# A RetNet and FoX decoder step on one core: value rows folded per head, state pairs spread over the value, head and gate steps

## What is computed

```python
def retention_mixer(h, pos, S0, w_in, w_out):
    q, k, v, g = split(h @ w_in)               # 1024, 1024, 2048, 2048 columns
    q, k = rotary(q, pos), rotary(k, pos) * RET_DK ** -0.5
    ...
    inner = einsum('bhij,bjhv->bihv', einsum('bihd,bjhd->bhij', q, k) * decay, v)
    cross = einsum('bihd,bhdv->bihv', q * q_dec, S)
    S_new = exp(L * log_gamma) * S + einsum('bjhd,bjhv->bhdv', k * k_dec, v)
    o = inner + cross
    ...
    o = o * rsqrt(mean(o * o) + EPS)           # over the 512 values of a head
    return (o * silu(g)) @ w_out, S_new
```

## Time and profile before

| what | us |
|---|---|
| median of 3 runs | 1557.9 |
| lowest and highest run | 1551.91, 1560.46 |
| the profiled execution, its time | 1551.63 |
| the profiled execution, its span | 1549.6 |
| start and modulation, until the q/k slots | 0 to 48.7 |
| q/k slots | 48.7 to 105.7 |
| value slots | 105.7 to 170.5 |
| value fold and past sums | 170.5 to 183.0 |
| heads | 183.0 to 273.6 |
| gate stage | 273.6 to 361.8 |
| modulation slots of `m0c` | 361.8 to 376.6 |
| output projection | from 376.6 |

### The profile page before, as it was taken

How to read it: one execution, slowest core, us unless ns; L and a number is a source line. 1 busy time by engine, 2 the same in 40 slices (tenths; PEclk the granted TensorE clock), 3 DMA queues, 4 the chain that set the end, 5 groups by cost and what they waited for, 6 DMA issues and landing times.

```text
span 1549.6 us, 19019 instructions
## 1 busy us (share of the span) xinstructions
PE 1373.4 (89%) x6290; PEld 748.9 (48%) x6290; DVE 634.6 (41%) x1678; ACT 244.4 (16%) x516; POOL 121.9 (8%) x234
## 2 busy tenths in 40 slices
PE   5999865988988999999899879989889889999995
PEld 3787532656864443434576723323324644334343
DVE  1220333331034344444400187687781253535354
ACT  2000233321022000000210121121220130000001
POOL 3330131320000000000000001111110000000000
PEclk8999986998998999999899956696799979999998
DMA  9764264997474999999953346666663629999992
GB/s 378 298 217 154 83 243 178 351 393 313 155 317 186 391 406 405 408 405 414 401 213 123 116 163 218 225 249 226 242 229 128 271 109 364 398 408 405 399 413 108
DMA packets 77032, 430.16 MB, mean 278 GB/s; under 512 B 9832, under 2 KB 11128, under 8 KB 38432
## 3 DMA queue, kind: packets, MB, share of 16 engines
q1 hardware_dynamic: 52704, 347.72, 57.1%
q0 software_dynamic: 23200, 76.10, 13.7%
q10 hardware_dynamic: 1056, 5.36, 0.9%
HBM read 406.94 MB, written 22.20 MB: 277 GB/s over the span
## 4 chain that ended last, share of the span: by engine, by line
PE 62%; DVE 9%; DMA 5%; issue 3%; ACT 2%; DVEq 1%; POOL 0%; SPq 0%; POOLq 0%
PE bank L778 60%; DMA ring<-wstream 3%; DVE arena L2107 2%; DVE arena L1943 1%; DVE h L2103 1%; DMA arena<-state 1%; PE bank L834 1%; DVE x L1959 1%; DVEq L1938 1%; DMA xn<-v_rows 1%; ACT arena L1492 1%; DVE arena L1972 1%; ACT xn L1381 0%; PE bank L792 0%; PE bank L1297 0%
## 5 line engine op out<-in xcount | busy, mean ns | idle before, releaser
L778 PE MATMUL bank<-arena 128*128 128x264 f32 (+7 forms) x1216 | 405.3, 518 | 61.4 <-ACT arena L1363 30.1
L778 PE MATMUL bank<-ring,arena 128*64 128x512 f32 (+3 forms) x1856 | 390.8, 560 | 7.6 <-issue 5.8
L778 PEld LDWEIGHTS bank<-arena 128*128 128x128 f32 (+4 forms) x1216 | 168.7, 166 | 274.9 <-issue 171.5
L778 PEld LDWEIGHTS bank<-ring,arena 128*64 128x64 f32 (+3 forms) x1856 | 141.9, 137 | 237.5 <-issue 213.8
L1363 ACT ACTIVATE arena<-bank 128x512 f32<-128x512 f32 (+6 forms) x186 | 85.8, 471 | 531.1 <-PE bank L778 432.1
L778 PE MATMUL bank<-h,ring 128*128 128x264 f32 x640 | 149.0, 394 | 0.5 <-DMA ring<-wstream 0.5
L778 PEld LDWEIGHTS bank<-h,ring 128*128 128x128 f32 x640 | 122.6, 193 | 30.1 <-issue 9.3
L1959 DVE SCALAR_TENSOR_TENSOR x<-bank,mod,x 128x256 f32<-128x256 f32 x256 | 119.3, 475 | 0.0
L778 PE MATMUL bank<-arena,ring 128*128 128x264 f32 x512 | 117.3, 393 | 0.8 <-DVE arena L2186 0.8
L778 PE MATMUL bank<-arena,cst 16*128 16x128 f32 (+8 forms) x210 | 82.2, 503 | 32.3 <-DVE arena L2168 19.9
L778 PEld LDWEIGHTS bank<-arena,ring 128*128 128x128 f32 x512 | 98.9, 194 | 18.7 <-DVE arena L2186 0.9
(11 more groups left out here) (229 smaller groups left out, 865.2 us busy)
## 6 DMA issues: line engine op xcount, KB each, us to landing
ring<-wstream SPq DMA_DIRECT2D x296, 1024.0 KB, 8.5
arena<-vcache POOLq DMA_DIRECT2D x64, 512.0 KB, 5.2
arena<-kcache SPq DMA_DIRECT2D x64, 512.0 KB, 4.7
arena<-state POOLq DMA_DIRECT2D x32, 512.0 KB, 9.4
ss_out<-arena POOLq DMA_DIRECT2D x32, 512.0 KB, 8.6
xn<-v_rows POOLq DMA_DIRECT2D x32, 256.0 KB, 8.8
sp_out<-arena ACTq DMA_DIRECT2D x4, 512.0 KB, 2.7
cst<-consts SPq DMA_DIRECT2D x1, 2005.5 KB, 22.2
```

Of the source, the lines that this page charges most:

```text
L778: ins = nc.tensor.matmul(out, w, rhs, start=start, stop=stop, skip_group_check=True)
```

## The change

- The value rows of the samples are folded per head (`("vfold", hd)`), behind the prompt values of slots 2, 4 and 6 of the stage and after the last, and are stored per head; `vpart` shrinks to one head, and `vb` has three buffers instead of four, so POOL issues the broadcast of u + 3 behind the store of u.
- The past sums move from behind the value stage to behind its first slot.
- Pairs 0 to 3 are read behind value slots 4 to 7 (`AT_V`, counted from 0), pairs 4 to 11 in the heads (`AT_HEAD`), pairs 12 to 15 in the first four gate steps (`AT_G`). ACT's scaling moves along: pairs 0 to 5 in the value stage, one pair ahead of `head_root` and one behind it in each head, pairs 14 and 15 in the gate stage.
- DVE updates the second pair of a head behind `head_scale`, no longer ahead of it.
- `outputs_turn` of head 0 stands ahead of head 1's scores, that of head 1 in head 2, the others in gate steps 0 and 4; the samples' norm is taken in gate step 5.
- At the start the small tensors are issued ahead of x, and the rest of the constants behind slot 11. POOL's first state loads wait for the first row of `m0b`.

```diff
+AT_V = {4: 0, 5: 1, 6: 2, 7: 3}
+AT_HEAD = {0: (4, 5), 1: (6, 7), 2: (8, 9), 3: (10, 11)}
+AT_G = {0: 12, 1: 13, 2: 14, 3: 15}
...
-        t.add(("vs", i), (X0, X1)[i % 2])
-    t.add("vfold", X0)
-    t.add(("past", 0), X0)
-    t.add(("past", 1), X1)
-    t.add("past_total", X0)
+        if i and i % 2 == 0:
+            t.add(("vfold", i // 2 - 1), X0)
+        t.add(("vs", i), X2)
+        if i == 0:
+            t.add(("past", 0), X0)
+            t.add(("past", 1), X2)
+            t.add("past_total", X0)
+        if AT_V.get(i) == 0:
+            t.add(("os", 0), X1)
+    t.add(("vfold", 3), X0)
...
-        root_o = rot.rearrange("p a b -> p (a b)")[:, 2 * T:2 * T + 2 * TP].rearrange("p (r n) -> p r n", r=2)
+        osb = rot.rearrange("p a b -> p (a b)")[:, RV:2 * RV]
+        root_o = ret.take(1, TP)
         vr = rot.rearrange("p a b -> p (a b)")[:, 0:RV]
-        vb = xn[:, :, :].rearrange("p a b -> p (a b)")[:, 0:4 * RV].rearrange("p (r n) -> p r n", r=4)
+        vb = xn[:, :, :].rearrange("p a b -> p (a b)")[:, RV:4 * RV].rearrange("p (r n) -> p r n", r=3)
...
+            sp.dma_start(cst[:, 0:N_EARLY], consts[:, 0:N_EARLY]).then_inc(consts_in, 16)
+            sp.dma_start(vec[:], vecs).then_inc(consts_in, 16)
             sp.dma_start(x[:], x_in).then_inc(x_loaded, 16)
-            sp.dma_start(cst[:, 0:N_EARLY], consts[:, 0:N_EARLY]).then_inc(consts_in, 16)
             for r in range(R):
                 sp.dma_start(ring[:, r, :], wstream[r]).then_inc(slot_in[r], 16)
-                if r == 0:
-                    sp.dma_start(vec[:], vecs).then_inc(consts_in, 16)
-            sp.dma_start(cst[:, N_EARLY:], consts[:, N_EARLY:]).then_inc(rest_in, 16)
-            sp.dma_start(wsm[:], wsmall).then_inc(rest_in, 16)
+            def rest_of_constants():
+                sp.dma_start(cst[:, N_EARLY:], consts[:, N_EARLY:]).then_inc(rest_in, 16)
+                sp.dma_start(wsm[:], wsmall).then_inc(rest_in, 16)
...
-            stream(R, S_MOE0 + 3 * NE)
+            for n in range(R, S_RET):
+                sp.wait_ge(slot_used, n - R + 1)
+                sp.dma_start(ring[:, n % R, :], wstream[n]).then_inc(slot_in[n % R], 16)
+            rest_of_constants()
+            stream(S_RET, S_MOE0 + 3 * NE)
...
+            moved(pool, ("row", "m0b", 0))
             for u in range(SB):
                 pool.dma_start(st[:, u, :, :], state[state_of(u)]).then_inc(state_in[u], 16)
 
+            def store_values(hd):
+                moved(pool, ("vfold", hd))
+                pool.dma_start(v_rows[hd], vr[MW * hd:MW * hd + NS, :]).then_inc(v_stored, 16)
+
             def values_everywhere(u):
-                pool.dma_start(vb[:, u % 4, :], v_rows[u // NS, u % NS:u % NS + 1, :].to_broadcast([P, RV])) \
-                    .then_inc(vb_in[u % 4], 16)
-
-            moved(pool, "vfold")
-            for hd in range(RH):
-                pool.dma_start(v_rows[hd], vr[MW * hd:MW * hd + NS, :]).then_inc(v_stored, 16)
-            pool.wait_ge(v_stored, 16 * RH)
-            for u in range(4):
+                if u % NS == 0:
+                    pool.wait_ge(v_stored, 16 * (u // NS + 1))
+                pool.dma_start(vb[:, u % 3, :], v_rows[u // NS, u % NS:u % NS + 1, :].to_broadcast([P, RV])) \
+                    .then_inc(vb_in[u % 3], 16)
+
+            store_values(0)
+            for u in range(3):
                 values_everywhere(u)
             for u in range(NS * RH):
 
@@ -691,12 +708,14 @@
                 else:
                     pool.wait_ge(state_read, 3 * (u // NS) + u // 2 % 4 + 1)
                 pool.dma_start(ss_out[state_of(u)], st[:, u % SB, :, :]).then_inc(state_out[u % SB], 16)
-                if u + 4 < NS * RH:
-                    values_everywhere(u + 4)
+                if u + 3 < NS * RH:
+                    values_everywhere(u + 3)
                 nxt = u + 5
                 if SB <= nxt < NS * RH:
                     pool.wait_ge(state_out[nxt % SB], 16 * (nxt // SB))
                     pool.dma_start(st[:, nxt % SB, :, :], state[state_of(nxt)]).then_inc(state_in[nxt % SB], 16)
+                if u % NS == 3 and u // NS + 1 < RH:
+                    store_values(u // NS + 1)
 
...
+                    mm(ps[:], ones, prev[:, i * 512:(i + 1) * 512], False, True, full)
+                ps, full = begin("past_total")
+                mm(ps[:, 0:NS * FH], ones, past_sum.rearrange("p b h -> p (b h)"), True, True, full)
+
             pe.wait_ge(hs_ready, 1)
             for i in range(8):
                 take_slot(S_RET + 8 + i)
                 values("v", None, S_RET + 8 + i, h, i)
+                if i and i % 2 == 0:
+                    fold_values(i // 2 - 1)
                 samples_in(("vs", i), S_RET + 8 + i)
-                mm(ps[MW * hd:MW * hd + MW, :], c_("fold"), vpart[:, hd * RV:(hd + 1) * RV], True, True,
-                   full if hd == RH - 1 else None)
-            pe.wait_ge(rest_in, 32)
...
+                if i == 0:
+                    past_sums()
+                if i in AT_V:
+                    read_states(AT_V[i])
+            fold_values(3)
...
             head_scores(0)
+            outputs_turn(0)
             for hd in range(RH):
                 if hd + 1 < RH:
                     head_scores(hd + 1)
                 head_output(hd)
                 if hd == 2:
-                    outputs_turn(0)
-                read_states(2 * hd)
+                    outputs_turn(1)
+                read_states(AT_HEAD[hd][0])
                 head_norm(hd)
-                read_states(2 * hd + 1)
+                if len(AT_HEAD[hd]) > 1:
+                    read_states(AT_HEAD[hd][1])
...
-                if i in (0, 4, 7):
-                    outputs_turn({0: 1, 4: 2, 7: 3}[i])
-                if i == 6:
-                    read_states(14)
+                if i in (0, 4):
+                    outputs_turn({0: 2, 4: 3}[i])
+                if i == 5:
+                    samples_norm()
                 columns(("g", i, 1), n, 1, h)
-                if i < 7:
-                    read_states(8 + i if i < 6 else 15)
-
-            mods("m0c", 0, 2)
...
+            def scale_pair(p):
+                scale_state(2 * p)
+                scale_state(2 * p + 1)
+
+            for i in range(8):
+                for c in range(2):
+                    ps = result(act, ("v", i, c))
+                    copy(vtok[:, c, i * 256:(i + 1) * 256], ps[:, 0:256]).then_inc(free(("v", i, c)), 1)
+                if i >= 2:
+                    scale_pair(i - 2)
+            sample_rows(0)
...
                 for s in range(2):
                     ps = result(act, ("rs", hd, s))
                     copy(sp_sb[:, s, :], ps[:]).then_inc(free(("rs", hd, s)), 1)
+                scale_pair(6 + 2 * hd)
                 moved(act, ("rs", hd, 1))
                 act.dma_start(sp_out[hd], sp_sb).then_inc(sp_stored, 16)
-                if hd >= 2:
-                    act.wait_ge(o_scaled, hd - 1)
+                if hd:
+                    act.wait_ge(o_scaled, hd)
                 head_root(hd)
-                for u in range(4 * hd + 4, min(4 * hd + 8, 18)):
-                    scale_state(u)
                 if hd == 1:
-                    act.wait_ge(v_stored, 16 * RH)
-                    sample_rows(0)
-            sample_rows(1)
+                    sample_rows(1)
+                scale_pair(7 + 2 * hd)
+            sample_rows(2)
...
+                if i < 2:
+                    scale_pair(14 + i)
                 if i == 3:
-                    sample_rows(2)
-                if i == 6:
                     sample_rows(3)
+                if i == 5:
+                    root_s = norm_s[:, 0, :, :]
+                    moved(act, "sam_norm")
+                    nc.scalar.activation(root_s, root_s, ACT.Sqrt, bias=eps, scale=1.0 / RV).then_inc(sam_rooted, 1)
+            mods("m0c")
...
+            def move_states(p):
+                for u in (2 * p, 2 * p + 1):
+                    hd, b = u // NS, u % NS
+                    dve.wait_ge(vb_in[u % 3], 16 * (u // 3 + 1))
+                    dve.wait_ge(state_scaled, u + 1)
+                    for s in range(2):
+                        ins = stt(st[:, u % SB, s, :], vb[:, u % 3, :], qk[:, 8 + 2 * hd + s, TP + b:TP + b + 1],
+                                  st[:, u % SB, s, :], ALU.mult, ALU.add)
+                    ins.then_inc(state_moved, 1)
...
+            for i in range(8):
+                if i and i % 2 == 0:
+                    rows_out(i // 2 - 1)
+                ps = result(dve, ("vs", i))
+                nc.vector.tensor_copy(vpart[:, i % 2 * 256:i % 2 * 256 + 256], ps[:, 0:256]).then_inc(free(("vs", i)), 1)
+                if i + 1 in AT_V:
+                    move_states(AT_V[i + 1])
+            rows_out(3)
...
             head_in(0)
+            samples_out(0)
             for hd in range(RH):
                 if hd + 1 < RH:
                     head_in(hd + 1)
```

(17 more changed lines are left out.)

186 lines of the change are left out of this document (80 added, 106 removed).

## The result

The changed kernel takes 1625.84 us (median of 4 runs, 1618.79 to 1630.18) against 1557.08 us before (4 runs): the ratio is 1.0438, with an interval of 1.0409 to 1.0467. It is slower, as forecast, but by 69 us and not by 50; 1625.84 lies 1.8 us above the upper end of the range. The profiled execution took 1618.79 us, its span is 1616.8.

The account below looks back on a forecast made before the run. TensorE, busy 89% of the span, was taken as the bound, so its idle time shows. Terms 1.5 + 0 + 11 + 59.6 - 12 - 8.6 - 1 = +50.5 us on 1551.6 gave 1602, as median 1608; range 1576 to 1624.

Parts of the forecast that it names:

- start, to the value stage: Reordered first transfers: q/k slots start at 48.7 again, but PE idles longer before them and restarts at half clock; +1.5 us.
- value stage: Takes over past sums, four reads, one zeroing and folds, 12.5 us, which go behind it; inputs arrive in time; 0, upper end +10.
- head 0, to the end of its first read: The turn ahead of head 1's scores waits 7.2 us for state 11, runs at half clock, then a slow restart; +11 us.
- first to second read, four heads: Inside each head: state load, root, reciprocal and product, updates and read take 17.9 us instead of 3.0; +59.6 us.
- second read to the next head's first: Between heads: the next head's last state is now the first load behind the second read, not the third; -12 us.
- gate stage: 79.5 us instead of 88.1, counting a 6.5 us wait for sample rows and three broadcast waits of some 1.5; -8.6 us.
- modulation slots: Behind the gate stage: they find a full ring and no norm in between, 14.8 becomes some 13.8 us; -1 us.
- main term: Inside each head, ScalarE scales a state let in by that head's first read before the root, delaying the second read; +59.6 us.
- rival 2: Value stage, three value buffers: broadcasts land in 9 to 11 us, PE waits 3 to 4 at three reads; +10, 1618; chance 0.08.
- B to A: From a head's second read to the next head's first: 65 us before, 53 after, turn and zeroing included; -12 us.
- Rival 1: At nine waits, state loads land 3.6 us from issue, each wait 3.6 shorter; +18, so 1576 us; chance 0.14.
- Rival 3: Retention stages: all state trips hide behind PE's work, so the kernel gets faster; -21, so 1537 us; chance 0.05.

Follow-up runs that it names:

- before_split: The kernel before with only the heads' reordering (two states scaled ahead of `head_root`, second pair updated behind `head_scale`): 1599.39 us, ratio 1.0253 to the kernel before.
- root_first: The changed kernel with ScalarE scaling pair 6+2hd behind `head_root` instead of ahead of it: 1595.32 us, ratio 1.0228 to the kernel before.
- lag: The changed kernel with ScalarE scaling each pair one pair later throughout, still three value buffers: 1550.01 us, ratio 0.9964 to the kernel before.
- four_buffers: The changed kernel with a fourth value buffer, GpSimd issuing the broadcast of u+4 behind the store of u: 1606.52 us, ratio 1.0312 to the kernel before.

## Why the prediction was right or wrong

| term | forecast | measured |
|---|---|---|
| start, to the value stage | +1.5 | +3.3 |
| value stage | 0 | +5.1 |
| head 0, to the end of its first read | +11 | +11.3 |
| first to second read, four heads | +59.6 | +59.8 |
| second read to the next head's first | -12 | -10.7 |
| gate stage | -8.6 | -2.7 |
| modulation slots | -1 | +0.8 |
| sum | +50.5 | +66.9 |

**The mechanism and its main term were right.** The stretch from read to read is 18.2, 18.2, 18.1 and 17.8 us (from 216.1 to 234.3, and so on), where the sum had 17.9. All four long waits are released by VectorE's update, the first turn waits 6.62 us (forecast 7.2), the past sums at 117.03 come without a wait. `before_split` and `root_first` show the mechanism by putting it in and taking half of it out, and in `lag`, where no state that ScalarE needs is let in by the last read, the trips are gone.

**The step that failed is the value stage's "0", with the waits of the gate stage.** Two thirds of the 16 us that are missing are there, and it is one thing in both: the second broadcast of a pair, issued only after the read before it because there are three buffers. The sum let it land 7.4 us after that read and had 8.8 against 8.4 us of work, which by itself is a wait of 0.4 at each of three reads and was put at nothing. It landed 8.4 us after (read done at 156.8, VectorE on at 165.2), and with 1.4 of updates that is 9.8 against 8.2 of work. The 6.4 came from the heads, where no weight slot travels. In the value stage they take 7.5 to 7.7 us. This was rival 2, with a chance of 0.08, and it gave 3 to 4 us at three reads; the waits are 1.71, 1.10 and 1.80, and 0.88 us for VectorE's copy of the last fold, which the sum didn't have. So its size was half, but it came twice, in the value stage and in the gate stage. There the forecast had three waits of 1.5 (measured 6.6 in all) and a turn's wait of 6.5 (7.58), since a state load among weight slots takes 9.29 us and not 7.2, and 2.7 us more of PE at the low clock behind these waits. `four_buffers` gives 13.7 us of the two stages back, which is more than the whole miss in them (5.1 + 5.9).

**The rest is small.** At the start the q/k slots begin 0.9 us later and take 59.4 us at a clock of 0.96, where they took 57.0 at 1.00: 3.3 in all, against 1.5 for a restart. The cause that the prediction gives, PE idle for longer before them (7.48 us), isn't shown: in `before_split` they take 59.0 us at 0.97 with no wait right ahead of them. Part of the 3.3 is chance, since the kernel before happened to start its value stage earliest of all. The modulation slots still wait for the ring, 1.86 us now and 1.64 before, which the forecast had dropped. B to A missed by 1.3.

**The median.** I put the forecast 6.3 above the profiled time, as it was before. This time the profiled execution lay 7.1 below the median again, but that was luck: in the twelve kernels of the experiments it lies between 12.0 us below and 12.6 above.

**Head 0** came out right (+11.3 for +11) from two errors that cancel: the turn waited 6.62 us and not 7.2, and the slow restart behind it cost 2.8 and not 2.

**Rival 1** (loads that land fast, at 3.6 us) is out. The Trainium skill, "DMA: Bandwidth & Descriptors", section "Anatomy of one DMA — SWDGE (gpsimd) path", gives a fit of 2.0 us plus bytes over 436 GB/s per DMA. Counting three transfers as one was the prediction's own step, and the estimate worked out so was 5 us from the store's issue to the load's landing. Measured are 1.06 + 7.6 = 8.7 us. With the broadcast moved away, the same estimate over 1 MB is 4.4 us; measured are 0.53 + 5.7 = 6.2. The measurement decides: here a store, a broadcast and a load in one queue don't add up as one transfer of their bytes.

**Rival 3** has a slip in its sum. Its parts for read B to read A, three times 11.7 and 3.5 for the turn and the zeroing, are 38.6 us and give -26 against 65, not -28. Nothing hangs on it.

## What to carry to other kernels

When a pipeline's step is moved one place earlier, ask which release its input now hangs on; here one place (`scale_pair(6 + 2 * hd)` for `5 + 2 * hd`, and the other scalings with it) was the difference between +4.4% and -0.4%. Take landing times from the stage in which the transfer will travel, and where a buffer is removed, compare its trip there with the work between two uses to within a microsecond. In a queue that issues store, broadcast and load, put first what somebody waits for, and look at what is then late instead.
